# Decay sums of a head pair as one 512-column product, the samples' scores made for all heads at once

## What is computed

```python
acum = jnp.cumsum((dt * a).reshape(b, nc, chunk, H), axis=2)
causal = jnp.tril(jnp.ones((chunk, chunk), bool))[None, None, :, :, None]
seg = acum[:, :, :, None, :] - acum[:, :, None, :, :]
decay = jnp.where(causal, jnp.exp(jnp.where(causal, seg, 0.0)), 0.0)
scores = jnp.einsum('bclhn,bcshn->bclsh', ch, bh) * decay
y_diag = jnp.einsum('bclsh,bcshp->bclhp', scores, xdt)
...
return (y_diag + y_off).reshape(b, L, H, P), h_final
...
y = y.astype(h.dtype) + lw['d_skip'][:, None] * xs
```

## Time and profile before

| what | value |
|---|---|
| median of 3 runs | 1817.0 us |
| the 3 runs | 1814.78, 1817.00 and 1824.93 us |
| the profiled execution, its own time | 1806.59 us |
| its span, first to last instruction | 1804.6 us |
| TensorE busy | 1687.1 us (93% of the span) |
| VectorE busy | 984.0 us (55%) |
| ScalarE busy | 635.7 us (35%) |
| mean granted TensorE clock | 0.964 of 2.4 GHz |

### The profile page before, as it was taken

How to read it: one execution, slowest core, us unless ns; L and a number is a source line. 1 busy time by engine, 2 the same in 40 slices (tenths; PEclk the granted TensorE clock), 3 DMA queues, 4 the chain that set the end, 5 groups by cost and what they waited for, 6 DMA issues and landing times.

```text
span 1804.6 us, 32096 instructions
## 1 busy us (share of the span) xinstructions
PE 1687.1 (93%) x13926; PEld 1526.3 (85%) x13926; DVE 984.0 (55%) x1248; ACT 635.7 (35%) x658; POOL 53.6 (3%) x151
## 2 busy tenths in 40 slices
PE   5999999998899978889959999999999999999997
PEld 3887888886677746578849999999999999999997
DVE  2434545453666435445485566555655656556566
ACT  2443222221444332142453433333333333333344
POOL 3000000001000000100000000000000000000000
PEclk9899999999899968899979999999999999999999
DMA  9787797988699961477725455555545544444441
GB/s 339 272 296 273 276 336 278 335 311 315 230 338 360 367 226 37 140 251 278 276 91 166 158 166 167 166 168 166 167 165 164 164 163 164 164 163 164 164 140 71
DMA packets 183077, 389.51 MB, mean 216 GB/s; under 512 B 7635, under 2 KB 16067, under 8 KB 182641
## 3 DMA queue, kind: packets, MB, share of 16 engines
q1 hardware_dynamic: 179488, 375.68, 60.2%
q0 software_dynamic: 2752, 9.24, 1.5%
q10 hardware_dynamic: 698, 2.55, 0.4%
HBM read 377.03 MB, written 10.41 MB: 215 GB/s over the span
## 4 chain that ended last, share of the span: by engine, by line
PE 82%; DVE 6%; DMA 6%; ACT 3%; issue 2%; SPq 0%; ACTq 0%; DVEq 0%
PE ps L804 15%; PE ps L803 15%; PE ps L802 15%; PE ps L783 7%; PE ps L785 6%; PE ps L784 6%; PE ps L724 4%; PE ps L763 4%; DMA raw<-in_w_in_dram 3%; PE ps L988 2%; PE ps L1021 1%; DVE wlo L1759 1%; DMA h<-in_state_ssm_dram 1%; PE ps L735 1%; PE ps L1184 1%
## 5 line engine op out<-in xcount | busy, mean ns | idle before, releaser
L1759 DVE TENSOR_TENSOR wlo<-raw,whi 128x2048 fp32r<-128x2048 f32 x146 | 332.9, 2288 | 194.2 <-ACT whi L1405 192.6
L1405 ACT ACTIVATE whi<-raw 128x2048 fp32r<-128x2048 f32 x145 | 277.6, 1915 | 431.9 <-PE ps L804 370.2
L804 PE MATMUL ps<-h2hi,wlo 128*128 128x288 f32 x1392 | 414.8, 298 | 0.0
L802 PE MATMUL ps<-h2hi,whi 128*128 128x288 f32 x1392 | 411.4, 296 | 0.8 <-DVE wlo L1759 0.8
L803 PE MATMUL ps<-h2lo,whi 128*128 128x288 f32 x1392 | 411.3, 296 | 0.0
L803 PEld LDWEIGHTS ps<-h2lo,whi 128*128 128x128 f32 x1392 | 262.9, 189 | 0.0
L802 PEld LDWEIGHTS ps<-h2hi,whi 128*128 128x128 f32 x1392 | 261.5, 188 | 1.0 <-DVE wlo L1759 1.0
L804 PEld LDWEIGHTS ps<-h2hi,wlo 128*128 128x128 f32 x1392 | 261.5, 188 | 0.0
L783 PE MATMUL ps<-hhi,whi_in 128*128 128x288 f32 x704 | 209.9, 298 | 4.3 <-ACT ctxT L1420 4.3
L784 PE MATMUL ps<-hlo,whi_in 128*128 128x288 f32 x704 | 209.3, 297 | 0.0
L785 PE MATMUL ps<-hhi,wlo 128*128 128x288 f32 x704 | 209.2, 297 | 0.0
(11 more groups left out here) (423 smaller groups left out, 2284.8 us busy)
## 6 DMA issues: line engine op xcount, KB each, us to landing
raw<-in_w_ffn_in_dram SPq DMA_DIRECT2D x88, 1024.0 KB, 5.0
raw<-in_w_ada_dram SPq DMA_DIRECT2D x84, 1024.0 KB, 8.5
raw<-in_w_in_dram SPq DMA_DIRECT2D x44, 1024.0 KB, 5.4
raw<-in_w_ffn_out_dram SPq DMA_DIRECT2D x44, 1024.0 KB, 5.0
kring<-in_cache_k_dram SPq DMA_DIRECT2D x64, 512.0 KB, 5.9
vring<-in_cache_v_dram SPq DMA_DIRECT2D x64, 512.0 KB, 5.5
raw<-in_w_out_dram SPq DMA_DIRECT2D x14, 1024.0 KB, 7.4
araw<-in_w_ada_dram SPq DMA_DIRECT2D x8, 1024.0 KB, 18.6
```

What stands on the lines that cost most here:

```text
L802: mm(o, high[:, q, cols], xh, start=(first and q == 0), stop=False)
L804: i = mm(o, low[:, q, cols], xh, start=False, stop=(last and q == QC - 1))
L1405: fn(high_of(g), landed_at(u), ACT.Copy).then_inc(hi_ready, 1)
L1759: tt(low_of(u), landed_at(u), high_of(g).bitcast(F32), SUB).then_inc(lo_ready, 1)
```

## The change

- `decay_sums(c)` becomes one product of 512 columns. The operands change places: the stationary one is now the constant `later`, and `steps` (now `incl` times `dt * a`) is the moving one, both heads and both chunks in one go, into one bank (`4 * (c % 2)`).
- The samples leave the loop. `steps_s` and the new `sco_s` hold all 16 heads, [32, 16, 32]. `sample_sums` (one 512-column product on 32 rows, into bank 1) is issued after `decay_sums(1)`; ScalarE's exp of it goes to `sco_s` after the second `dec`; `weigh_samples` on VectorE multiplies it in place by `cbm`, after `diag_out(2)`; `y_samples` (16 products of 32 columns) is issued after the last `y_diag`.
- `dec`, `sco` and `diag_out` cover 256 columns of a head instead of 288. The samples' `xc` x skip factor for all pairs is one VectorE instruction in the loop's fifth turn, and the product is added by another behind the loop.
- Each shared semaphore counts one more event, placed between pairs, so the waits of later pairs add one.
- GpSimd's zeroing of `cbm` and its semaphore go; VectorE waits for `ov_lo` itself.

```diff
-        steps_s = [at(f"steps_s{k}", [TS, 2, TS], WREG + 4096 + 256 * k) for k in range(2)]
+        steps_s = at("steps_s", [TS, HS, TS], WREG + 4096)
+        sco_s = at("sco_s", [TS, HS, TS], WREG + 30080)
...
-        dec, sco = ([at(f"{n}{k}", [P, 2, T], WREG + off) for k, off in enumerate(o)]
+        dec, sco = ([at(f"{n}{k}", [P, 2, NT, P], WREG + off) for k, off in enumerate(o)]
...
-            pool.wait_ge(ov_lo, 1)
-            pool.memset(cbm[:], 0.0).then_inc(cbm_zeroed, 1)
...
             def decay_sums(c):
-                pe.wait_ge(steps_ready, c + 1)
+                pe.wait_ge(steps_ready, c + 1 + (c >= 2))
                 if c >= 2:
-                    pe.wait_ge(dec_ready, c - 1)
-                for a in range(2):
-                    bank = 4 * (c % 2) + a
-                    for t in range(NT):
-                        mm(ps[:, bank, t * P:(t + 1) * P], steps[c % 2][:, a, t, :], incl[:], start=True, stop=True)
-                    i = mm(ps[0:TS, bank, SEQ:T], steps_s[c % 2][:, a, :], incl_s[:], start=True, stop=True)
-                i.then_inc(seg_full, 1)
+                    pe.wait_ge(dec_ready, c - 1 + (c >= 4))
+                mm(ps[:, 4 * (c % 2), :], later[:], steps[c % 2][:].rearrange("p a t i -> p (a t i)"),
+                   start=True, stop=True).then_inc(seg_full, 1)
+
+            def sample_sums():
+                pe.wait_ge(steps_ready, 3)
+                mm(ps[0:TS, 1, :], later_s[:], steps_s[:].rearrange("p h i -> p (h i)"), start=True, stop=True)\
+                    .then_inc(seg_full, 1)
 
             def y_diag(c):
-                pe.wait_ge(sco_ready, c + 1)
+                pe.wait_ge(sco_ready, c + 1 + (c >= 4))
                 if c >= 2:
                     pe.wait_ge(yd_out, c - 1)
-                for t in range(NT + 1):
-                    w = P if t < NT else TS
+                for t in range(NT):
                     for a in range(2):
                         h = 2 * c + a
...
+            def y_samples():
+                pe.wait_ge(sco_ready, 5)
+                for c in range(SC):
+                    for a in range(2):
+                        h = 2 * c + a
+                        i = mm(ps[a * PD:(a + 1) * PD, 1, c * TS:(c + 1) * TS], xdt_tok[0:TS, NT, h * PD:(h + 1) * PD],
+                               sco_s[:, h, :], start=True, stop=True)
                 i.then_inc(yd_full, 1)
 
             decay_sums(0)
             decay_sums(1)
+            sample_sums()
             for c in range(SC):
                 if c + 2 < SC:
                     decay_sums(c + 2)
                 y_diag(c)
+            y_samples()
...
-                fn(dec[k % 2][:], ps[:, 4 * (k % 2):4 * (k % 2) + 2, 0:T], ACT.Exp).then_inc(dec_ready, 1)
+                fn(dec[k % 2][:].rearrange("p a t i -> p (a t i)"), ps[:, 4 * (k % 2), :], ACT.Exp).then_inc(dec_ready, 1)
+                if k == 1:
+                    act.wait_ge(seg_full, 3)
+                    fn(sco_s[:].rearrange("p h i -> p (h i)"), ps[0:TS, 1, :], ACT.Exp).then_inc(dec_ready, 1)
...
             for k in range(SC):
...
                     steps_of(k + 2)
                 if k:
                     diag_out(k - 1)
+                if k == 3:
+                    weigh_samples()
+                if k == 4:
+                    c.mark(tt(yT[:, :, SEQ:T], xc[:, 0:SC, SEQ:T], dskE[:].unsqueeze(2).to_broadcast([P, SC, TS]), MUL))
             diag_out(SC - 1)
-            dve.wait_ge(yd_out, SC)
+            dve.wait_ge(yd_full, SC + 1)
+            c.settle()
+            tt(yT[:, :, SEQ:T], yT[:, :, SEQ:T], ps[:, 1, 0:SC * TS].rearrange("p (c x) -> p c x", c=SC), ADD).then_inc(yd_out, 1)
+            dve.wait_ge(yd_out, SC + 1)
```

More of the change, by code:

```diff
@@ L339, in hybrid_step @@
         g2 = sem("g2")
-        cbm_zeroed = sem("cbm_zeroed")
         seg_full, steps_ready, dec_ready, sco_ready, yd_full, yd_out = (
@@ L1118, in decay_sums @@
             def decay_sums(c):
[L1121 removed]
+                pe.wait_ge(steps_ready, c + 1 + (c >= 2))
                 if c >= 2:
[L1123 to L1129 removed]
+                    pe.wait_ge(dec_ready, c - 1 + (c >= 4))
[5 more added lines that the diff above has]
+                    .then_inc(seg_full, 1)
             def y_diag(c):
[L1132 removed]
+                pe.wait_ge(sco_ready, c + 1 + (c >= 4))
                 if c >= 2:
                     pe.wait_ge(yd_out, c - 1)
[L1135 to L1136 removed]
+                for t in range(NT):
                     for a in range(2):
                         h = 2 * c + a
[L1139 to L1140 removed]
+                        i = mm(ps[a * PD:(a + 1) * PD, 2 + c % 2, t * P:(t + 1) * P], xdt_tok[:, t, h * PD:(h + 1) * PD],
+                               sco[c % 2][:, a, t, :], start=True, stop=True)
+                i.then_inc(yd_full, 1)
+            def y_samples():
[5 more added lines that the diff above has]
+                               sco_s[:, h, :], start=True, stop=True)
                 i.then_inc(yd_full, 1)
@@ L1159, in _ @@
             i.then_inc(yo_full, 1)
-            pe.wait_ge(yd_out, SC)
+            pe.wait_ge(yd_out, SC + 1)
             pe.wait_ge(yo_out, 2)
@@ L2133, in steps_of @@
                 if k >= 2:
-                    dve.wait_ge(seg_full, k - 1)
+                    dve.wait_ge(seg_full, k - 1 + (k >= 4))
                 two = dA_tok[:, 0:NT, 2 * k:2 * k + 2].rearrange("p t h -> p h t").unsqueeze(3).to_broadcast([P, 2, NT, P])
-                tt(steps[k % 2][:], later[:].unsqueeze(1).unsqueeze(2).to_broadcast([P, 2, NT, P]), two, MUL)
-                tt(steps_s[k % 2][:], later_s[:].unsqueeze(1).to_broadcast([TS, 2, TS]),
-                   dA_tok[0:TS, NT, 2 * k:2 * k + 2].unsqueeze(2).to_broadcast([TS, 2, TS]), MUL).then_inc(steps_ready, 1)
+                tt(steps[k % 2][:], incl[:].unsqueeze(1).unsqueeze(2).to_broadcast([P, 2, NT, P]), two, MUL).then_inc(steps_ready, 1)
             dve.wait_ge(xdt_out, 3)
@@ L2145, in _ @@
                 .then_inc(xde_made, 1)
-            dve.wait_ge(cbm_zeroed, 1)
+            dve.wait_ge(ov_lo, 1)
             dve.wait_ge(B_full, 2)
@@ L2154, in _, with weigh_samples @@
             steps_of(1)
+            tt(steps_s[:], incl_s[:].unsqueeze(1).to_broadcast([TS, HS, TS]),
+               dA_tok[0:TS, NT, :].unsqueeze(2).to_broadcast([TS, HS, TS]), MUL).then_inc(steps_ready, 1)
             def weigh(k):
-                dve.wait_ge(dec_ready, k + 1)
+                dve.wait_ge(dec_ready, k + 1 + (k >= 2))
                 if k >= 2:
                     dve.wait_ge(yd_full, k - 1)
-                tt(sco[k % 2][:], dec[k % 2][:], cbm[:, k // GCH].unsqueeze(1).to_broadcast([P, 2, T]), MUL).then_inc(sco_ready, 1)
+                pair = lambda a: a.rearrange("p a t i -> p a (t i)")
+                tt(pair(sco[k % 2][:]), pair(dec[k % 2][:]), cbm[:, k // GCH, 0:SEQ].unsqueeze(1).to_broadcast([P, 2, SEQ]), MUL)\
+                    .then_inc(sco_ready, 1)
+            def weigh_samples():
+                dve.wait_ge(dec_ready, 3)
+                groups = sco_s[:].rearrange("p (g h) i -> p g h i", g=G)
+                tt(groups, groups, cbm[0:TS, :, SEQ:T].unsqueeze(2).to_broadcast([TS, G, HS // G, TS]), MUL).then_inc(sco_ready, 1)
             def diag_out(k):
                 dve.wait_ge(yd_full, k + 1)
-                stt(yT[:, k, :], xc[:, k, :], dskE[:, k:k + 1], ps[:, 2 + k % 2, 0:T], MUL, ADD).then_inc(yd_out, 1)
+                stt(yT[:, k, 0:SEQ], xc[:, k, 0:SEQ], dskE[:, k:k + 1], ps[:, 2 + k % 2, 0:SEQ], MUL, ADD).then_inc(yd_out, 1)
             dve.wait_ge(cbm_made, 1)
```

4 lines of the change are left out of this document (2 added, 2 removed).

## The result

Over 20 executions each, the changed kernel has a median of 1809.54 us (1801.84 to 1818.04), the kernel before 1820.24 us (1809.91 to 1833.22): a ratio of 0.9944, with a 95% interval of 0.9924 to 0.9963, that is 6.7 to 13.8 us faster, 10.2 us at the ratio itself. The forecast was 1813.3 us and a gain of 3.7 us. The two profiled executions, however, are alike: 1806.59 us before, 1806.41 us after.

The account below looks back on a forecast made before the run. TensorE was taken to bound the old loop, VectorE the new; stepping the engines' costs moved the loop's end from 699.32 to 695.6, a 3.7 us gain from the 1817.0 us median, so 1813.3 us, range 1804 to 1821.

Parts of the forecast that it names:

- The loop at full clock: Loop over pairs: some 17.2 us from first decay-sum product to the product behind the loop, instead of 20.9, at clock 1.00.
- the stepping: Loop over pairs: three engines stepped through the listed order with trace occupancies and 0.1 us hand-overs; old loop's end 699.5.
- The drain: TensorE in the loop: a change of tiling mode drains it, 0.17 us; each turn loses four of its six shape changes.
- The gain doesn't travel: Rival, behind the loop: a load starting by its own time ends the chain; result 1817 us, chance 0.05.
- The sequence loop: Rival, sequence loop: earlier arrival changes its clock phase, up to 4 us either way, 1809 or 1817 us; chance 0.17.
- The size: Whole kernel: gain of 3.7 us, all from the loop over pairs; 5.0 with costs at low ends, 1.4 at high.
- The clock rival: Rival, loop over pairs: TensorE, now waiting, falls to half clock; 3.3 us slower than before, 1820.3 us, chance 0.08.
- The scatter: Timed runs: median of three spans 10 us, profiled execution 10 us below it; over 0.5% faster gets chance 0.15.

Follow-up runs that it names:

- samples_grouped: Kernel before, with each turn's four 128-column decay sums issued first and its two 32-column ones behind them; ratio 0.9931, median 1804.3 us.
- placed: Changed kernel with the samples' weighing, skip product and final products moved into idle slots of the loop; ratio 0.9930 to the kernel before, median 1805.6 us.
- before_idle: Kernel before, with eight dummy VectorE products ahead of the first steps so TensorE idles before the loop; ratio 1.0065, median 1830.7 us.
- after_idle: Changed kernel with eight dummy VectorE products ahead of the first steps; ratio to the kernel before 0.9988, median 1815.9 us.
- four_idle: four_products with eight dummy VectorE products ahead of the first steps; ratio to the kernel before 0.9978, median 1814.9 us.
- four_products: Changed kernel with a pair's decay sums again as four 128-column products, samples still out of the loop; ratio to the kernel before 0.9942, median 1807.4 us.
- grouped_idle: samples_grouped with eight dummy VectorE products ahead of the first steps; ratio to the kernel before 0.9966, median 1814.1 us.

## Why the prediction was right and wrong

- **The loop at full clock: right.** 17.25 us against a forecast 17.2. The waits of VectorE came where the stepping had put them, ahead of the first, third and sixth `diag_out`: 0.61, 0.17 and 0.82 us, 1.60 in all against a forecast 1.7. That the total fits to 0.05 us is luck, since two errors cancelled. The last `weigh` starts 14.87 us after the loop does, instead of 14.66: the product costs 1.06 us, not 0.92, where the 64-column `y_diag` follows (the first ones, with no change of shape behind them, take some 0.95). And `y_samples` costs 1.05, not 1.2. With TensorE at 1.64 us a turn and VectorE at 1.6 neither is the bound by itself, and the chain passes from one to the other, where the forecast named VectorE alone. The starts of `weigh` were to be 1.6 to 1.8 us apart; from the third on (687.72) they are 1.6 to 1.9, and 2.5 where `weigh_samples` stands between.
- **The drain: right.** By samples_grouped each change of shape costs 0.15 us, close to the 0.17 of the earlier trace rows. The Trainium skill's rule (TensorEngine Tiling (Array Packing), Key Properties) stands with that number. It carries most of what TensorE's turn gained, 0.81 us (2.45 to 1.64): four changes of shape make an estimated 0.60, if the two that samples_grouped leaves in cost 0.15 too; the samples' short products themselves 0.18 (2.15 to 1.67, less two changes); the width 0.03. A turn of the old loop has four array shapes, 128*128, 32*32, 128*64 and 32*64, not three as the text ahead of the prediction says; the six changes are right.
- **"The gain doesn't travel": didn't happen.** From the first product behind the loop to the start of the output projection (L783, then L780) there are 64.8 us before and 64.3 after.
- **The sequence loop: a scatter, not an effect of the change.** Between the first pair of profiles its clock changed phase (mean 0.85 instead of 0.83), but its length by under 1 us. Over all 14 profiles, however, the stretch from the first product of the new state (L1157 before) to the output projection takes 56.8 to 63.3 us. The same kernel shows 62.9 and 59.5, and the mean is 60.8 for the six with the old kind of loop and 60.4 for the eight with the new. So the rival's size, up to 4 us either way, was about right, and a single profiled time can hide or feign a gain of this size.
- **The size: wrong, by a factor of nearly three.** The step that failed is the base of the sum: the old loop was priced at 20.9 us because the one profiled execution showed that. In its two profiles it is 20.9 and 32.1 us. Counted from the state product and with the slower products behind it (3.58 us from the first L1152 to the first L1157 instead of 1.89), a fallen clock costs the old kernel 12.7 us. By the clocks of the 100 timed executions about six in ten had it, and they are 13.8 us slower in the median. The changed loop loses 1.6 us where the old one loses 11. So the gain over a slow execution of the old kernel is some 14 us, and the 10 between the medians are mostly that. Whether the loop's own 3.6 us arrive is not shown: the 37 executions of the old kernel with the higher clock have a median of 1809.6 us, the 32 of the changed kernel one of 1809.1.
- **The clock rival: right mechanism, wrong kernel.** Its reasoning was that TensorE, now waiting in each turn, might lose the clock. "Before, gaps of up to 1.16 us did not keep the clock from 1.00" was read from one execution; in another the clock fell 2 us after such a gap, in a loop without any. In samples_grouped and placed, with the same gap and nearly the same time of arrival, it stayed at 1.00. The Trainium skill, TensorE: Matmul & The Clock Gate, section HAM oscillation, ties the fall to TensorE's idling between bursts of matmuls, in its example in waits for DMA; the prediction's "exactly such a fall" says more than that for waits of 0.2 to 1 us. No idling was needed to stay at half clock here: the loop of before_idle, busy 33.5 of 33.7 us, never rose.
- **The scatter.** The prediction noted that the profiled execution lay 10 us below the median and took it for scatter that only widens a range. It was, for the larger part, the trace of the mechanism. The range held (1804 to 1821 us), but the forecast 3.7 us lies outside the measured interval of 6.7 to 13.8. That 1813.3 us comes within 4 us of 1809.5 is partly luck: the gain is 6.5 to 7 us too small, and the base, 1817.0 as the median of three executions, is 3.2 us below the 1820.2 of twenty. A gain of over 0.5% got a chance of 0.15; measured is 0.56% (0.37 to 0.76%).

Left open: when the old loop falls to half clock (no run varied its start finely), and the 4 us by which the stage begins later. Of the six profiled kernels with the old kind of loop five reached the state product between 672 and 674.1 us; of the eight with the new kind two did, and six reached it between 676 and 679.4. The order of the work ahead of it is the same but for GpSimd's zeroing of `cbm` (at 664.55), and 2.9 of the 4.2 us between the first two profiles are there before that: the products of `small` and `sel` start at 632.6 and 635.5. If it is not chance, it takes back a part of the gain in the changed kernel; no run tested it.

## What to carry to other kernels

A gap of 10 us between the profiled time and the median of the runs was a finding here, not noise: profile the unchanged kernel a second time before pricing a change to it, and compare the granted clock stage by stage. Where every timed execution has its mean clock, plot that against the time: two clusters are two kinds of execution. A stage of short products in several array shapes can sit at half clock while TensorE is never idle. Group products by shape, take the small ones out, and look at what stands ahead of the stage as well as at its work. If a stage's time is in doubt, make its start slow and fast on purpose (idle time ahead of it, dummy wide products ahead of it): the two ends bound what the change can be worth.

## What the runs showed of the hardware

- The granted clock was not decided by TensorE's busy share alone. Busy for 33.5 of 33.7 us with short products that change shape six times a turn, it stayed at 1.2 GHz (before_idle). Busy to the same degree with 512-column products it rose within 3.8 us (after_idle), with 128-column ones without the samples' after some 9 and 4.5 us (four_idle, four_products), grouped by shape after some 12 us (grouped_idle).
- One program can have its executions in two clusters: the same loop took 20.9 us at a clock of 1.00 and 32.1 us at 0.50 but for its first 2 us.
- Work can be added for a gain: 7.3 us of unused products made the kernel 8.7 us faster by the median.
- A change of array shape costs 0.15 us (samples_grouped), and 32 records of 32-row, 64-column products with 32 moving columns take 1.05 us, 0.033 us each.
